# Joining four weight units at three entries, an earlier table load in attention, and VectorE low halves in one gate stage

## What is computed

```python
for l in range(DEPTH):                      # DEPTH = 2
    hl = modulate(x, ml[..., 0, :], ml[..., 1, :])
    zl = hl @ w_in[l] + b_in[l]             # q, k, v, conv halves, pool, three gates
    q_l, k_l, v_l = qkv_heads(zl, q_gain[l], k_gain[l])
    ...
    attn_l = latent_attention(q_l, k_l, v_l, k_c, v_c)
    x = layer_norm(DEEPNORM_ALPHA * x + ml[..., 2, :] * mix(zl, attn_l), ln1_g[l], ln1_b[l])
    x = layer_norm(DEEPNORM_ALPHA * x + ml[..., 5, :] * ffn(modulate(x, ml[..., 3, :], ml[..., 4, :])), ln2_g[l], ln2_b[l])

def conv_ffn(h, w_up, dw_w, dw_b, w_down):  # D_FF = 2816
    a, u = jnp.split(h @ w_up, 2, axis=-1)
    a = depthwise_conv(a, dw_w, dw_b)       # 3 taps
    return (jax.nn.silu(a) * u) @ w_down
```

## Time and profile before

| | |
|---|---|
| time, median of 3 runs | 3250.37 us (3248.43 to 3252.75) |
| profiled execution: time, span | 3252.26 us, 3250.5 us |
| granted TensorE clock, mean | 0.991 of full speed |
| PE busy | 3130.7 us, 96% of the span |
| DVE busy | 1959.5 us, 60% |
| ACT busy | 1139.8 us, 35% |
| POOL busy | 847.2 us, 26% |
| HBM traffic | 83 GB/s mean over the span |

### The profile page before, as it was taken

How to read it: one execution, slowest core, us unless ns; L and a number is a source line. 1 busy time by engine, 2 the same in 40 slices (tenths; PEclk the granted TensorE clock), 3 DMA queues, 4 the chain that set the end, 5 groups by cost and what they waited for, 6 DMA issues and landing times.

```text
span 3250.5 us, 43690 instructions
## 1 busy us (share of the span) xinstructions
PE 3130.7 (96%) x16074; PEld 2483.6 (76%) x16074; DVE 1959.5 (60%) x2691; ACT 1139.8 (35%) x1616; POOL 847.2 (26%) x332
## 2 busy tenths in 40 slices
PE   7999999999989999998999999999999999999998
PEld 4778877888878888886777677868886786777775
DVE  4787887664566254356878975774636565245443
ACT  3122254234233221123333535343223536343543
POOL 0001200233323233231012024434444322333312
PEclk9999999999999999999999999999999999999999
DMA  7442100112111211124541012322223111122211
GB/s 280 171 164 78 40 14 27 45 59 98 64 46 59 65 64 60 64 67 144 182 140 52 1 65 84 131 73 97 96 91 113 66 65 52 65 84 72 85 39 65
DMA packets 75308, 270.52 MB, mean 83 GB/s; under 512 B 8592, under 2 KB 9616, under 8 KB 74512
## 3 DMA queue, kind: packets, MB, share of 16 engines
q1 hardware_dynamic: 71376, 256.04, 23.2%
q10 hardware_dynamic: 3776, 12.32, 1.1%
HBM read 263.87 MB, written 4.46 MB: 83 GB/s over the span
## 4 chain that ended last, share of the span: by engine, by line
PE 83%; DVE 10%; DVEq 2%; ACT 2%; issue 2%; DMA 1%; ACTq 0%; SPq 0%
PE ps L551 49%; PE ps L857 11%; PE ps L517 4%; PE ps L667 2%; PE ps L790 2%; PE ps L998 1%; DVE arena L2083 1%; PE ps L688 1%; PE ps L655 1%; DVE x L2091 1%; PE ps L770 1%; PE ps L1077 1%; PE ps L600 1%; PE ps L558 1%; PE ps L1095 1%
## 5 line engine op out<-in xcount | busy, mean ns | idle before, releaser
L479 POOL TENSOR_TENSOR w_lo<-w_raw,w_hi 128x1024 fp32r<-128x1024 f32 x328 | 847.0, 2585 | 2367.7 <-ACT w_hi L1198 2367.5
L1198 ACT ACTIVATE w_hi<-w_raw 128x1024 fp32r<-128x1024 f32 x380 | 399.5, 1055 | 550.8 <-PE ps L551 299.6
L551 PE MATMUL ps<-act_hi,w_hi 128*128 128x512 f32 (+1 forms) x2608 | 552.5, 361 | 2.1 <-DVE x L1931 0.6
L551 PE MATMUL ps<-act_lo,w_hi 128*128 128x512 f32 (+1 forms) x2608 | 535.4, 354 | 0.0
L551 PE MATMUL ps<-act_hi,w_lo 128*128 128x512 f32 (+1 forms) x2608 | 534.6, 354 | 0.0
L551 PEld LDWEIGHTS ps<-act_hi,w_hi 128*128 128x128 f32 x2608 | 428.0, 188 | 119.9 <-issue 47.4
L551 PEld LDWEIGHTS ps<-act_lo,w_hi 128*128 128x128 f32 x2608 | 428.2, 188 | 71.9 <-issue 0.5
L551 PEld LDWEIGHTS ps<-act_hi,w_lo 128*128 128x128 f32 x2608 | 428.1, 188 | 72.0
L1931 DVE SCALAR_TENSOR_TENSOR x<-ps,mod,x 128x512 f32<-128x512 f32 x96 | 60.3, 659 | 290.8 <-PE ps L551 238.2
L2091 DVE SCALAR_TENSOR_TENSOR x<-arena,vec,x 128x512 f32<-128x512 f32 x336 | 230.6, 714 | 0.2 <-issue 0.2
L2083 DVE SCALAR_TENSOR_TENSOR arena<-arena,vec 128x783 f32<-128x783 f32 (+1 forms) x240 | 228.1, 950 | 0.0
(11 more groups left out here) (336 smaller groups left out, 4399.0 us busy)
## 6 DMA issues: line engine op xcount, KB each, us to landing
w_raw<-in_weights SPq DMA_DIRECT2D x380, 512.0 KB, 3.4
arena<-in_ada_w SPq DMA_DIRECT2D x75, 512.0 KB, 4.9
tmp<-in_ada_w SPq DMA_DIRECT2D x21, 512.0 KB, 5.4
x<-in_x SPq DMA_DIRECT2D x2, 1536.0 KB, 20.0
x<-in_x ACTq DMA_DIRECT2D x1, 3072.0 KB, 10.3
arena<-in_pool_w ACTq DMA_DIRECT2D x2, 1024.0 KB, 4.9
x_mid<-x ACTq DMA_DIRECT2D x1, 2048.0 KB, 7.4
x<-x_mid ACTq DMA_DIRECT2D x1, 2048.0 KB, 8.4
```

What stands on the lines that cost most here:

```text
L479: nc.gpsimd.tensor_tensor(WL[:, w], raw, WH[:, w].bitcast(f32), ALU.subtract).then_inc(units_split, 1)
L551: last = nc.tensor.matmul(ps(t, a, b), w[:, s * UNIT + k * P:s * UNIT + (k + 1) * P], act[:, k * TOK + a:k * TOK + b], start=(n == 0 and k ...
L1198: nc.scalar.activation(WH[:, s * UNIT:(s + 1) * UNIT], RAW[:, (s % 2) * UNIT:(s % 2 + 1) * UNIT], ACT.Copy).then_inc(hi_done, 1)
```

## The change

1. **`up0`, both layers.** `first_four` takes the place of `first_pair` and the two units behind it. For the first 5 chunks (first layer) or 6 (second) the products of all four units are done together, chunk by chunk, each in a tile of its own; then each unit is finished in turn. `up0` as a whole uses tile s for slot s.
2. **`conv` in the second layer.** The same with the four units in two tiles, slots 2 and 3 in the second bank of tiles 0 and 1; the four small products of `ada_ahead` come after the four.
3. **V stage, both layers.** `head_norm` of the last head stands behind t == 2 and no longer behind t == 0.
4. **Attention, both layers.** ACT's two high halves at the entry move behind attention, in front of the load of `pool_w`. The table set that exp needs is loaded ahead of the loop and not by the first exp.
5. **`up0` in the second layer.** DVE makes the 16 low halves refilled in its loop (`refill_low`), slot 2u behind the taps, slot 2u+1 behind `scale_chunk`; POOL leaves these four rounds out.

```diff
-        STAGES += [((_l, f"up{_p}"), _n // 2, (_n, _n, 0, 0)), ((_l, f"down{_p}"), 2, (0, 0, 4, 4))]
+        STAGES += [((_l, f"up{_p}"), _n // 2, (_n // 2,) * 4 if _p == 0 else (_n, _n, 0, 0)), ((_l, f"down{_p}"), 2, (0, 0, 4, 4))]
...
-            for r0, r1 in ((RING[0, "qkv"] + 1, RING[1, "conv"] + 1), (RING[1, "qkv"] + 1, ROUNDS)):
+            for r0, r1 in ((RING[0, "qkv"] + 1, RING[1, "conv"] + 1), (RING[1, "qkv"] + 1, RING[1, "up0"] + 1),
+                           (RING[1, "up0"] + 1 + FF_PARTS[0] // 2, ROUNDS)):
...
+                def first_four():
+                    together = kt - (3 if len(sp_) > 1 else 2)
+
+                    def products_of(s, n, k):
+                        w, act = ((WH, hi), (WL, hi), (WH, lo))[n]
+                        if n != 1 and s == 0:
+                            pe.wait_ge(*at_least(l, ready[n // 2][0], ready[n // 2][1] + k + 1))
+                        for a, b in sp_:
+                            last = nc.tensor.matmul(tile(0, s, a, b), w[:, s * UNIT + k * P:s * UNIT + (k + 1) * P],
+                                                    act[:, k * TOK + a:k * TOK + b],
+                                                    start=(n == 0 and k == 0), stop=(n == 2 and k == kt - 1))
+                        return last
+
+                    for k in range(together):
+                        for n in range(3):
+                            for s in range(SLOTS):
+                                if k == 0 and n == 0:
+                                    start(0, s)
+                                products_of(s, n, k)
+                    for s in range(SLOTS):
+                        for k in range(together, kt):
+                            for n in range(3):
+                                last = products_of(s, n, k)
+                        last.then_inc(units_used, 1)
+                    if ahead:
+                        for s in range(SLOTS):
+                            ahead(s)
...
-                linear(l, "conv", 4, sp_, ready=(("h_hi", 0), ("h_lo", 0)), ahead=lambda u: ada_ahead(l, u))
+                linear(l, "conv", 4, sp_, ready=(("h_hi", 0), ("h_lo", 0)), ahead=lambda u: ada_ahead(l, u), four="banks" if l else None)
...
-                    if t == 0:
+                    if t == 2:
                         head_norm(l, KV_HEADS + HEADS - 1)
...
-                for s in (2, 3):
-                    refill(l, "qkv", 2, s)
...
+                nc.scalar.preload_act_table_set("natural_log_exp_and_others")
                 act.drain()
                 heads("attn", 0, 4, 6)
                 if l == 0:
                     heads("attn_ctx", SEQ, 2, 2)
+                for s in (2, 3):
+                    refill(l, "qkv", 2, s)
                 act.dma_start(AR[:, POOLW:POOLW + 2048], pool_w[l]).then_inc(on(l, "pool_w"), 16)
...
+            def refill_low(i, r, s):
+
+                w = slice(s * UNIT, (s + 1) * UNIT)
+                dve.wait_ge(hi_done, i * SLOTS + (r * SLOTS + s + 1))
                 V.tensor_tensor(WL[:, w], RAW[:, (s % 2) * UNIT:(s % 2 + 1) * UNIT], WH[:, w].bitcast(f32), ALU.subtract).then_inc(units_split, 1)
...
                             t.then_inc(on(l, "ff_conv"), 1)
+                            if refills:
+                                refill_low(i, RING[l, "up0"] + 1, 2 * u)
...
                             if p == 0:
                                 scale_chunk(l, "ln1", "ln1_g", i * 2 + u, W)
+                            if refills:
+                                refill_low(i, RING[l, "up0"] + 1, 2 * u + 1)
```

More of the change, by code:

```diff
@@ L489, in _, with linear, tile @@
         def _(pe):
-            def linear(l, st, rounds, sp_, kt=CH, hi=XH, lo=XL, ready=None, ahead=None, behind=None, within=None, by_chunk=False, tb=0):
+            def linear(l, st, rounds, sp_, kt=CH, hi=XH, lo=XL, ready=None, ahead=None, behind=None, within=None, by_chunk=False, tb=0,
+                       four=None):
+                def tile(i, s, a, b):
+                    if four == "slots":
+                        return ps(s, a, b)
+                    if four == "banks":
+                        return ps(s % 2, s // 2 * 512 + a, s // 2 * 512 + b)
+                    return ps(tb + s % 2, a, b)
                 def start(i, s):
                     pe.wait_ge(units_split, unit_done(l, st, i, s))
-                    pe.wait_ge(tile_free[tb + s % 2], taken(l, st, tb + s % 2, use(i, s)))
+                    if four == "slots":
+                        pe.wait_ge(tile_free[s], taken(l, st, s, i))
+                    elif four == "banks":
+                        pe.wait_ge(tile_free[s % 2], taken(l, st, s % 2, max(use(i, s) - 1, 0)))
+                    else:
+                        pe.wait_ge(tile_free[tb + s % 2], taken(l, st, tb + s % 2, use(i, s)))
                 def single(i, s):
@@ L503, in single @@
                         return unit_by_chunk(l, s, tb + s % 2, sp_).then_inc(units_used, 1)
-                    unit(s, tb + s % 2, sp_, kt, hi, lo, within if within and i * SLOTS + s == CH - 1 else None).then_inc(units_used, 1)
+                    unit(s, lambda a, b: tile(i, s, a, b), sp_, kt, hi, lo, within if within and i * SLOTS + s == CH - 1 else None).then_inc(units_used, 1)
                     if behind:
@@ L542, in linear, with unit @@
                             single(i, s)
-            def unit(s, t, sp_, kt, hi, lo, within=None):
+            def unit(s, tile, sp_, kt, hi, lo, within=None):
                 for n, (w, act) in enumerate(((WH, hi), (WL, hi), (WH, lo))):
@@ L550, in unit @@
                         for a, b in sp_:
-                            last = nc.tensor.matmul(ps(t, a, b), w[:, s * UNIT + k * P:s * UNIT + (k + 1) * P],
+                            last = nc.tensor.matmul(tile(a, b), w[:, s * UNIT + k * P:s * UNIT + (k + 1) * P],
                                                     act[:, k * TOK + a:k * TOK + b],
@@ L830, in block1 @@
                     first = sum(FF_PARTS[:p])
[L831 removed]
+                    linear(l, f"up{p}", n // 2, sp_, ready=(("h2_hi", 0), ("h2_lo", 0)) if p == 0 else None,
+                           four="slots" if p == 0 else None)
                     linear(l, f"down{p}", 2, sp_, n, GH, GL, ready=(("g_split", first), ("g_split", first)), tb=2,
@@ L2305, in block1 @@
                     Wf = W + (1 if l == 0 else 0)
+                    refills = l == 1 and p == 0
+                    if refills:
+                        dve.wait_ge(units_split, (RING[l, "up0"] + 1) * SLOTS)
                     with dve.Fori(0, n // 2) as i:
```

33 lines of the change are left out of this document (20 added, 13 removed).

## The result

The changed kernel takes 3231.52 us (median of 4 runs, 3231.39 to 3232.3), the kernel before 3251.56 us in the same comparison (4 runs, 3248.43 to 3256.64). The ratio is 0.9939, with a 95% interval of 0.9927 to 0.9951: 20.0 us faster, between 16 and 24. The forecast was 3229, a gain of 21.2, in the range 3221 to 3241.

What follows compares the result with a forecast made beforehand. PE, busy 96% of the span, was taken to bound the kernel, so gains come only from its waits or slow clock. Gains of 25.0 less costs of 3.8 gave net 21.2 us: 3250.37 to 3229, range 3221 to 3241.

Steps and rivals of the forecast that it cites:

- the wait at the old line 813: PE's wait at the mixing behind attention; above 3 us would show the prediction wrong.
- V stage: First layer: PE's 4.10 us wait and the slow clock behind it vanish, 26.66 to 19.32 us; gain 7.3.
- up0 entry, first layer: Four joined units remove 3.88 us of PE waits and some 2 of half clock; gain 5.9 us.
- conv entry: Second layer: four joined units remove 3.27 us of waits and a little clock; gain 3.8 us, 2 to 4.5.
- up0 entry, second layer: Waits of 3.82 us and the clock, less some 0.4 for DVE's low half; gain 4.1 us, 3 to 5.
- Attention's entries: Exp 1.3 us earlier and DVE's scaling undisturbed by POOL; gains 2.3 us first layer, 1.6 second.
- Waits at down0: down0's first pair waits for DVE to empty tile 3; cost 1.3 us first layer, 1.0 second.
- Behind attention, second layer: Two added POOL operations delay DVE by 2.0 us each, partly absorbed by idle time; cost 1.5 us, 0 to 4.
- Part 5, DVE's low halves: Second layer's up0: DVE needs 7.1 to 8 us a pair against PE's 10.9, so stays off the path.
- My rival for this stage: Second layer's up0: DVE becomes late, the entry's 4.1 us is lost; gain 17 us, 3233; chance 0.08.
- given back: Rival: exit stall at full 4 us plus half clock, longer tile waits, conv gains only 2; 3239 us; chance 0.17.
- the others: Rivals: DVE late in second up0 (0.08), drain saved (0.05), slower (0.03), nothing (0.02), interleaving costs PE (within 0.17).

Runs made afterwards that it cites:

- e9: The changed kernel run again with no edit, as same-chip partner for two later runs; 3234.99 us, ratio 0.9944.
- e1: Changed kernel with the last head's norm put back behind t == 0; 3240.76 us, ratio 0.9967.
- e6: Changed kernel with the second layer's conv back to two units first; 3236.46 us, ratio 0.9955.
- e4: Changed kernel with up0 back to two units first and two tiles in both layers, DVE's low halves kept; 3242.2 us, ratio 0.9968.
- e3: Changed kernel without the table load ahead of the loop, leaving it to the first exp; 3233.26 us, ratio 0.9947.
- e7: Changed kernel with the table load ahead of the last copy of V and the high halves behind that copy, both layers; 3233.33 us, ratio 0.9944.
- e2: Changed kernel with ACT's two high halves back at attention's entry, table load behind them, both layers; 3234.44 us, ratio 0.9947.
- e8: Changed kernel with up0 using only tiles 0 and 1 from the fifth unit on; 3234.27 us, ratio 0.9949.
- e10: Changed kernel with DVE, not POOL, making the two moved units' low halves ahead of the second layer's gating; 3232.71 us, ratio 0.9937.
- e5: Changed kernel with POOL making the low halves in the second layer's up0 again; 3239.16 us, ratio 0.9963.
- e11: Changed kernel with earlier table load, second-layer high halves at attention's entry, their low halves in DVE's idle time, up0 later on two tiles; 3229.31 us, ratio 0.9930.

## Why the prediction was right

The sum was 21.2 and 20 came out, and most terms held one by one. That the total came so near is in part luck: the exit cost 2.5 us more than its term, and the first layer's `up0` entry gained 1.4 more than its own, since the clock recovered sooner than in the kernel before. In e9, the same kernel, it gained 6.0.

Of the signs of being wrong that the prediction named, one came true, the wait at the old line 813: 3.25, where it said above 3. It belongs to the term that was mis-sized, below. PE also waits once within `up0` for `w_lo`, 0.53 at the second layer's unit 4, for which the sum had 0.4.

- *V stage*: 7.3 forecast, 6.9 measured, e1 shows it alone (7.05) and that nothing came back later. DVE's idle time ahead of the first maximum is 3.4 us where it was 10.34, and the sum had left 3.
- *up0 entry, first layer*: 5.9 forecast, 7.3 in the first profile and 6.0 in e9. The term was right, the rest is when the clock recovers (0.96 mean over the entry where it was 0.89).
- *conv entry*: 3.8 forecast, 3.9 measured, and e6 loses 3.9 by it alone.
- *up0 entry, second layer*: 4.1 forecast, 4.3 measured; e4 shows it at 5.0 against its own.
- *Attention's entries*: 2.3 and 1.6 forecast, 2.7 and 1.4 measured. The sizes were right and the reason was half wrong. I added a table load out of the way (1.3) and an undisturbed scaling. e3 shows that the load is out of the way without the added line, e7 that an exp 1.3 us earlier gains nothing while POOL runs. What counts is when POOL's second operation ends. In the first layer 1.4 of 2.7 is that. The other 1.25 is the half clock at the scores (four matmuls in 2.93 and now 1.56), but its cause isn't shown. It came back in neither e1 nor e2, which each undo one of the two parts that stand ahead of it. In e2 PE waits 2.45 us ahead of these scores, as long as in the kernel before, and the clock stays full. Whether both parts together bring the fall, no run shows.
- *Waits at down0*: 1.3 and 1.0 forecast, 1.31 and 0.98 measured; e4 and e8 show that they are tile 3's.
- *Behind attention, second layer*: this term was mis-sized, 1.5 forecast (0 to 4), 4.0 measured. Each operation of POOL cost the gating 2.2 us (11.52 - 4.91 for three, of which one was there before, against the windows), so two added ones 4.4. DVE's idle time took about 1.8 of it and left 2.6, which is the growth of the wait (3.25 - 0.67). The other 1.4 is PE at the half clock behind the longer wait (5.15 and 3.70), and e10 shows it: with a wait of 1.64 it is 3.70 again. I had both pieces, the 2.0 for an operation and a clock that falls behind a wait of 2 us, and used the second only in a rival.
- *Part 5, DVE's low halves*: I priced it at nothing, in that DVE stays off the path, and that is right of the changed kernel: its first multiplies come 7.3 us apart, in the forecast 7.1 to 8, until PE sets the pace. But I forecast for e5 that POOL could do it as well, and that was wrong: it is what keeps the joined entry's gain. My rival for this stage had the wrong engine: DVE is late with POOL beside it and not with its own low halves.

The rival "given back" had the right mechanism at the exit and the wrong size elsewhere; the others didn't occur. The joined units run at 0.227 us a matmul (rows of four start 0.907 apart in `conv`), the 0.227 of the plain stage, so interleaving costs PE nothing. No wait on `hi_done` held DVE in the second layer's `up0`.

What stays open: what of the median's 1 to 4 us in several experiments is the start, since only one execution of each was profiled; what brought the half clock at the first layer's scores in the kernel before; the fall in the second block in e8 and e11; and why loops run at two speeds (below).

## What to carry to other kernels

Work moved off a critical entry must be followed to where it lands, on every engine that it triggers: here two high halves cost nothing on ACT, but the low halves that they release on POOL held DVE for 2.2 us each, wherever they ran beside DVE's SBUF work. Look for the idle time of the engine that will be disturbed, and put the work, or its consequence, there. And a stage that PE finishes earlier shortens the time in which slower engines catch up: a backlog that was hidden shows at the next tile.

## What the runs showed of the hardware

- DVE and POOL: a wide operation of DVE that takes all its inputs from SBUF is held until about the end of POOL's (2.81 us and not 0.62, e7; 2655 ns and not 692 for line 1852), one that reduces out of PSUM is not (0.96 us at 1748.60 in e7, in the midst of POOL's 4.65). The Trainium skill (SBUF — State Buffer, SBUF: two separate sides) has it as an exclusive lock for a whole instruction, taken by operations with two SBUF inputs or in a mode with two ports, and the rows agree.
- At a granted clock of 1.00 the same loop over a unit of 768 columns runs at two speeds. These are PE rows of 16 matmuls in `up0` of the first layer, first of the changed kernel, then of e8:

```profile
951.17 2.99 PE L595 MATMUL ps<-act_hi,w_lo 128*128 128x512 f32 x16
954.00 2.98 PE L595 MATMUL ps<-act_lo,w_hi 128*128 128x512 f32 x16
```

```profile
955.31 2.94 PE L597 MATMUL ps<-act_hi,w_lo 128*128 128x512 f32 x16
958.08 2.94 PE L597 MATMUL ps<-act_lo,w_hi 128*128 128x512 f32 x16
```

They start 2.83 apart in one and 2.77 in the other, 2%. It repeats for the same kernel (e9) and changes with edits elsewhere: the twelve units took 101.8 to 101.9 us in the kernels before and after, e2, e4, e9, e10 and e11, and 99.8 to 100.0 in e1, e3, e5, e6, e7 and e8. No run here tells why.
- The half clock does not begin at the same place of an equal wait. Ahead of the first layer's `up0` PE waited 6.03 us in both kernels. The granted clock was half from 922.5 to 929.3 before and from 909.1 to 915.9 after, 6.8 us each time. But before, 1.0 of these lay in the wait and 5.8 behind it, and after, 4.0 lay in it and 2.8 behind. The joined entry took 34.7 to 36.6 us in the changed kernel and the experiments that have it. The changed kernel alone took 35.3 and 36.6, so 1.3 us are the execution's.
